# GpSimd issues the next expert's gather ahead of its wait for the last scatter; tokens loaded first and normalised by a diagonal product

## The reference, cut to what matters

```python
def _rmsnorm(x, gain):
    y = xf * lax.rsqrt(jnp.mean(xf * xf, axis=-1, keepdims=True) + EPS)
    return y * gain

def _layer(x, ...):
    xn = _rmsnorm(x, p['norm_mix'])
    z = xn @ p['w_in']                       # u | q | f | i | g
    y_s5 = ...                               # diagonal state space scan, GELU, GLU, RMSNorm
    y_hg = ...                               # 8 heads of 128x128 state, chunked
    x = x + concat([y_s5, y_hg]) @ p['w_out']
    return x + _hier_moe(_rmsnorm(x, p['norm_ffn']), ...)

def _hier_moe(x, w_coarse, b_coarse, w_fine, b_fine, w_gate, w_up, w_down):
    # top-1 group of 4, then top-2 of its 8 experts: gate (n, 32) has two entries per token
    hg = einsum('nd,edf->nef', xs, w_gate)   # 32 experts, 2048 -> 512
    hu = einsum('nd,edf->nef', xs, w_up)
    act = silu(hg) * hu * gate[:, :, None]
    return einsum('nef,efd->nd', act, w_down)
```

## Time and profile before

| | |
|---|---|
| median of 3 runs | 1835.31 us (1832.76 to 1837.85) |
| profiled execution, time | 1835.85 us |
| profiled execution, span | 1834.0 us, 19193 instructions |
| TensorE busy, weight load busy | 1483.5 us (81%), 908.7 us (50%) |
| VectorE, ScalarE, GpSimd busy | 599.6 us, 274.4 us, 308.3 us |
| moved by DMA | 505.26 MB, mean 275 GB/s |
| of it the expert weights | 192 loads of 2 MB |

### The profile page before, as it was taken

The page is one execution under the profiler, slowest core; times in us unless marked ns, Lnnn a source line. Parts: engine busy times, 40 slices in busy tenths (PEclk is TensorE's granted clock), DMA queues, the critical chain, the costliest instruction groups (busy, mean ns, idle before and its releaser), DMA issues.

```text
span 1834.0 us, 19193 instructions
## 1 busy us (share of the span) xinstructions
PE 1483.5 (81%) x7437; PEld 908.7 (50%) x7437; DVE 599.6 (33%) x1466; ACT 274.4 (15%) x501; POOL 308.3 (17%) x426
## 2 busy tenths in 40 slices
PE   6799988879988997778878788787887878878870
PEld 5676666567766875434434334333343334433330
DVE  2779999956654124101010010100101001010015
ACT  1100001143331001110111111111011111111111
POOL 0055555433310010000000000000000000000006
PEclk9999998999998998887978888788888888888885
DMA  9323322344514564699999999999999999999954
GB/s 281 121 93 99 129 89 81 109 138 131 165 38 112 183 230 165 248 410 384 403 390 386 385 397 395 388 388 393 386 382 403 382 394 400 395 391 394 389 222 151
DMA packets 130318, 505.26 MB, mean 275 GB/s; under 512 B 23716, under 2 KB 99700, under 8 KB 102780
## 3 DMA queue, kind: packets, MB, share of 16 engines
q1 hardware_dynamic: 112908, 493.74, 70.1%
q0 software_dynamic: 5200, 9.19, 1.5%
q10 hardware_dynamic: 12160, 1.67, 0.6%
HBM read 503.19 MB, written 26.28 MB: 289 GB/s over the span
## 4 chain that ended last, share of the span: by engine, by line
PE 31%; DMA 27%; issue 5%; ACT 3%; DVE 2%; POOL 1%; POOLq 0%; ACTq 0%; SPq 0%; DVEq 0%
PE bank L1288 16%; DMA arena<-x_rows,idx_tok 15%; DMA expert_rows<-arena,idx_dst 11%; PE bank L1197 6%; PE bank L1234 5%; ACT arena L726 3%; PE bank L1267 2%; PE bank L906 1%; DVE arena L1794 1%; DMA ring<-expert_rows 1%; PE bank L1164 0%; PE bank L1147 0%; POOL arena L868 0%; POOL arena L861 0%; PE bank L1175 0%
## 5 line engine op out<-in xcount | busy, mean ns | idle before, releaser
L1267 PE MATMUL bank<-ring,arena 128*64 128x512 f32 x2048 | 450.5, 595 | 0.0
L1267 PEld LDWEIGHTS bank<-ring,arena 128*64 128x64 f32 x2048 | 227.1, 137 | 195.2 <-issue 195.2
L1288 PE MATMUL bank<-ring,arena 128*64 128x512 f32 x1024 | 292.6, 736 | 19.0 <-DVE arena L1794 19.0
L1234 PE MATMUL bank<-ident,arena 64*128 64x64 f32 x721 | 96.9, 326 | 189.1 <-DMA arena<-x_rows,idx_tok 185.2
L936 PE MATMUL bank<-arena,ring 128*128 128x280 f32 x768 | 195.6, 416 | 4.5 <-ACT arena L576 3.1
L1789 DVE SCALAR_TENSOR_TENSOR arena<-arena,gcol 64x512 f32<-64x512 f32 x32 | 35.6, 1113 | 499.2 <-ACT arena L721 499.2
L1234 PEld LDWEIGHTS bank<-ident,arena 64*128 64x128 f32 x721 | 90.5, 242 | 217.5 <-DMA arena<-x_rows,idx_tok 212.5
L1288 PEld LDWEIGHTS bank<-ring,arena 128*64 128x64 f32 x1024 | 87.4, 171 | 201.9 <-issue 201.9
L936 PEld LDWEIGHTS bank<-arena,ring 128*128 128x128 f32 x768 | 150.4, 198 | 48.7 <-issue 8.7
L845 POOL DMA_INDIRECT expert_rows<-arena,idx_dst x32 | 29.5, 921 | 779.5 <-ACT arena L726 779.5
L726 ACT ACTIVATE arena<-bank 64x512 f32<-64x512 f32 x128 | 75.9, 593 | 527.2 <-PE bank L1288 526.1
(11 more groups left out here) (334 smaller groups left out, 1435.5 us busy)
## 6 DMA issues: line engine op xcount, KB each, us to landing
ring<-in_w_down_dram SPq DMA_DIRECT2D x64, 2048.0 KB, 9.0
ring<-in_w_gate_dram SPq DMA_DIRECT2D x64, 2048.0 KB, 9.5
ring<-in_w_up_dram SPq DMA_DIRECT2D x64, 2048.0 KB, 15.3
ring<-in_w_in_dram SPq DMA_DIRECT2D x20, 2048.0 KB, 8.7
ring<-in_w_out_dram SPq DMA_DIRECT2D x8, 2048.0 KB, 9.4
ring<-in_s_w_glu_dram SPq DMA_DIRECT2D x2, 2048.0 KB, 8.3
arena<-v_samples SPq DMA_DIRECT2D x8, 512.0 KB, 4.2
ring<-expert_rows SPq DMA_DIRECT2D x4, 1024.0 KB, 10.6
```

The source lines that it names most:

```text
L1234: return pe.matmul(out, rows, eye, start=True, stop=True) if waits else pe.transpose(out, rows, eye)
L1267: ins = pe.matmul(PB[b][at:at + CAP, :], xgT[b][:, kk, :], slot(s, KD // 2)[:, k, :], start=(kk == 0), stop=(kk == KD - 1))
L1288: ins = pe.matmul(PB[2 + cc // 2][at:at + CAP, :], hT[:, f, :], slot(4 + half, KF // 2)[:, k, cc * 512:(cc + 1) * 512], start=(f == 0), st ...
```

## The change

In the loop, GpSimd's wait for a scatter and the raise of `rows_free` move behind the next gather. For x: wait for `tr_done`, gather x+1, wait for scatter x-1, raise `rows_free`, wait for `rows_ready`, scatter x. The first pair is written out ahead of the loop, since it has no earlier scatter, and the last scatter is waited for behind the loop.

In the head, the tiles are taken in the order 0, 1, 2 and all loaded before the vectors. The sum of squares of a tile is made in two halves of 1024 columns, one by ScalarE, one by VectorE, and added by VectorE. The tile is no longer scaled: VectorE writes the reciprocals into a diagonal matrix `diag`, and TensorE multiplies by that in place of the transpose.

```diff
--- before.py
+++ after.py
@@ -194,6 +194,7 @@
         q_own = c(NH, NS, NS)
         assert c.at <= 2 * SLOT
         c = Carver(upair, 0)
+        diag = c(3, P)
         xsq = c(D)
         ang_r, ang_n, ang_cos, ang_sin = (c(NJ, 33) for _ in range(4))
         z_tmp = [c(NS, NJ), c(NS, NJ)]
@@ -245,6 +246,8 @@
         idx_tok = [sb(f"idx_tok{i}", [CAP, 1], U32) for i in range(2)]
         idx_dst = [sb(f"idx_dst{i}", [CAP, 1], U32) for i in range(2)]
         gcol = [sb(f"gcol{i}", [CAP, 1]) for i in range(2)]
+        half_sums = sb("half_sums", [P, 3, 2])
+        HALF_SQ = D // 2
         rcol = [sb(f"rcol{i}", [CAP, 1]) for i in range(2)]
         square_sums = sb("square_sums", [P, 3, D // CB])
 
@@ -264,7 +267,7 @@
         vec_loaded, s5_loaded, bc_loaded, wr_loaded = sems("vec_loaded s5_loaded bc_loaded wr_loaded")
         slot_loaded = [sem(f"slot_loaded{i}") for i in range(6)]
         pool_consts, dve_consts, act_step, dve_step, pool_step = sems("pool_consts dve_consts act_step dve_step pool_step")
-        x_rms, xn_made, xt_done, xt_copied, vec_t, vec_copied = sems("x_rms xn_made xt_done xt_copied vec_t vec_copied")
+        x_half, x_summed, x_rms, xn_made, xt_done, xt_copied, vec_t, vec_copied = sems("x_half x_summed x_rms xn_made xt_done xt_copied vec_t vec_copied")
         lb_in, lb_exp = sems("lb_in lb_exp")
         s5_exp_in, s5_exp, s5_sin_in, s5_sin, s5r_ready = sems("s5_exp_in s5_exp s5_sin_in s5_sin s5r_ready")
         par_t, par_copied, ang_ready, table_ready = sems("par_t par_copied ang_ready table_ready")
@@ -415,11 +418,10 @@
                     rows = t[name].rearrange("a (k p) -> (a k) p", p=P)
                     sp.dma_start(vrow[at:at + rows.shape[0], :], rows).then_inc(vec_loaded, 16)
 
-            for tile in TILE_ORDER:
+            for tile in range(3):
                 for at, rows in token_rows(tile):
                     sp.dma_start(xraw[at:at + rows.shape[0], tile, :], rows).then_inc(x_loaded[tile], 16)
-                if tile == TILE_ORDER[0]:
-                    load_vectors()
+            load_vectors()
             for n in range(NW + PRE_SLOTS):
                 pre_load(n)
 
@@ -536,19 +538,16 @@
                     act.dma_start(h0row[:, z, half, :], src[half].rearrange("b j n -> (b j) n")).then_inc(s5_loaded, 16)
             step = Chain(act, act_step)
 
-            def token_rms(src, scratch, tile, signal):
-
-                n = TT[tile]
-                s = token_stats[0:n, tile:tile + 1]
-                step.link(nc.scalar.activation(scratch[0:n, :], src[0:n, tile, :], ACT.Square, accum_out=s))
-                nc.scalar.activation(s, s, ACT.Sqrt, bias=eps_col[0:n, :], scale=1.0 / D).then_inc(signal, 1)
-
-
             act.wait_ge(dve_consts, 1)
             nc.scalar.activation(token_stats[:, 7:8], eps_col[:, :], ACT.Sqrt)
-            for tile in TILE_ORDER:
+            for tile in range(3):
+                n = TT[tile]
                 act.wait_ge(x_loaded[tile], 16 * len(token_rows(tile)))
-                token_rms(xraw, xsq, tile, x_rms)
+                nc.scalar.activation(xsq[0:n, 0:HALF_SQ], xraw[0:n, tile, 0:HALF_SQ], ACT.Square,
+                                     accum_out=half_sums[0:n, tile, 0:1]).then_inc(x_half, 1)
+                act.wait_ge(x_summed, tile + 1)
+                nc.scalar.activation(token_stats[0:n, tile:tile + 1], token_stats[0:n, tile:tile + 1], ACT.Sqrt,
+                                     bias=eps_col[0:n, :], scale=1.0 / D).then_inc(x_rms, 1)
             for z, (bn, cn) in enumerate((("s5_B_re", "s5_C_re"), ("s5_B_im", "s5_C_im"))):
                 act.dma_start(Braw[z], t[bn][0].rearrange("(j g) p c -> (g p) j c", g=2)).then_inc(bc_loaded, 16)
                 act.dma_start(Craw[z], t[cn][0].rearrange("(i g) c p -> (g c) i p", g=8)).then_inc(bc_loaded, 16)
@@ -829,24 +828,36 @@
                                         in_offset=bass.IndirectOffsetOnAxis(ap=idx_tok[p][:, 0:1], axis=0),
                                         bounds_check=last_token, oob_is_err=False).then_inc(gathered[p], 16)
 
+            def pair_of_rows(R, i, first):
+
+                for b in range(2):
+                    x = i * 2 + (R * NE + b)
+                    g = i * 2 + (R * (NE + 1) + b + 1)
+
+                    pool.wait_ge(tr_done, g)
+                    gather(g, 1 - b)
+
+                    if b == 1:
+                        pool.wait_ge(scattered[0], i * 16 + (R * (NE // 2) + 1) * 16)
+                        pool.sem_inc(rows_free, 1)
+                    elif not first:
+                        pool.wait_ge(scattered[1], i * 16 + R * (NE // 2) * 16)
+                        pool.sem_inc(rows_free, 1)
+                    pool.wait_ge(rows_ready, x + 2)
+                    pool.sem_inc(wait_carried, 1)
+                    pool.indirect_dma_start(out=y_dram, out_offset=bass.IndirectOffsetOnAxis(ap=idx_dst[b][:, 0:1], axis=0),
+                                            in_=yout[b][0:CAP, :], in_offset=None, bounds_check=last_row,
+                                            oob_is_err=False).then_inc(scattered[b], 16)
+
             def round_rows(R):
                 if not is_first(R):
                     pool.wait_ge(tr_done, R * (NE + 1) + 1)
                 gather(R * (NE + 1), 0)
-                with pool.Fori(0, NE // 2) as i:
-                    for b in range(2):
-                        x = i * 2 + (R * NE + b)
-                        g = i * 2 + (R * (NE + 1) + b + 1)
-
-                        pool.wait_ge(tr_done, g)
-                        gather(g, 1 - b)
-                        pool.wait_ge(rows_ready, x + 2)
-                        pool.sem_inc(wait_carried, 1)
-                        pool.indirect_dma_start(out=y_dram, out_offset=bass.IndirectOffsetOnAxis(ap=idx_dst[b][:, 0:1], axis=0),
-                                                in_=yout[b][0:CAP, :], in_offset=None, bounds_check=last_row,
-                                                oob_is_err=False).then_inc(scattered[b], 16)
-                        pool.wait_ge(scattered[b], i * 16 + (R * (NE // 2) + 1) * 16)
-                        pool.sem_inc(rows_free, 1)
+                pair_of_rows(R, 0, True)
+                with pool.Fori(1, NE // 2) as i:
+                    pair_of_rows(R, i, False)
+                pool.wait_ge(scattered[1], (R + 1) * (NE // 2) * 16)
+                pool.sem_inc(rows_free, 1)
 
             run_rounds(pool, round_rows)
             pool.engine_nop().then_inc(moe_done, 1)
@@ -886,7 +897,7 @@
             pe.transpose(PB[7][:, 0:80], vrow[0:80, :], ident[0:80, 0:80]).then_inc(vec_t, 1)
 
 
-            for i, tile in enumerate(TILE_ORDER):
+            for i, tile in enumerate(range(3)):
                 n = TT[tile]
                 pe.wait_ge(xn_made, i + 1)
                 for q in range(KD // 4):
@@ -895,7 +906,8 @@
                         pe.wait_ge(xt_copied, unit - 3)
                     for a in range(4):
                         k = 4 * q + a
-                        ins = pe.transpose(PB[unit % 4][:, a * P:a * P + n], xraw[0:n, tile, k * P:(k + 1) * P], ident[0:n, 0:n])
+                        ins = pe.matmul(PB[unit % 4][:, a * P:a * P + n], xraw[0:n, tile, k * P:(k + 1) * P], diag[0:n, tile, 0:n],
+                                        start=True, stop=True)
                     ins.then_inc(xt_done, 1)
 
             def last_tile(bank, lhs, w):
@@ -1303,17 +1315,36 @@
             nc.vector.memset(square_sums[:, :, :], 0.0)
             nc.vector.memset(eps_col[:, :], EPS).then_inc(dve_consts, 1)
 
-            for i, tile in enumerate(TILE_ORDER):
+            def sum_squares(tile):
+
                 n = TT[tile]
-                dve.wait_ge(x_rms, i + 1)
+                dve.wait_ge(x_loaded[tile], 16 * len(token_rows(tile)))
+                half = xraw[0:n, tile, HALF_SQ:D]
+                step.link(STT(xsq[0:n, HALF_SQ:D], half, 1.0, half, ALU.mult, ALU.mult, accum_out=half_sums[0:n, tile, 1:2]))
+                dve.wait_ge(x_half, tile + 1)
+                TTo(token_stats[0:n, tile:tile + 1], half_sums[0:n, tile, 0:1], half_sums[0:n, tile, 1:2], ALU.add) \
+                    .then_inc(x_summed, 1)
+
+            def make_diag(tile):
+
+                n = TT[tile]
+                dve.wait_ge(x_rms, tile + 1)
                 r = token_stats[0:n, 3 + tile:4 + tile]
                 step.link(nc.vector.reciprocal(r, token_stats[0:n, tile:tile + 1]))
-                TS(xraw[0:n, tile, :], xraw[0:n, tile, :], r, None, ALU.mult).then_inc(xn_made, 1)
+                TS(diag[0:n, tile, 0:n], ident[0:n, 0:n], r, None, ALU.mult).then_inc(xn_made, 1)
+
+            dve.wait_ge(pool_consts, 4)
+            sum_squares(0)
+            sum_squares(1)
+            make_diag(0)
+            sum_squares(2)
+            make_diag(1)
+            make_diag(2)
             dve.wait_ge(vec_t, 1)
```

(2 more changed lines are left out.)

## The result

The changed kernel takes 1804.71 us (median of 4 runs, 1800.81 to 1807.39) against 1836.58 us for the kernel before (4 runs, 1832.76 to 1840.75): a ratio of 0.9828, interval 0.9806 to 0.985. It is faster, by about half of what was forecast, and 1.7 us beyond the upper end of the range. The profiled execution has a span of 1805.5 us (its own time 1807.39), 28.5 less than the 1834.0 of before.

A forecast was written before the change was run, and what follows sets the result against it. TensorE's late gathered rows kept the weight queue from staying full. From a span of 1834.0 us, 49.2 (loop), 7.7 (loop's end) and 3.0 (head) were taken, giving 1774.1; with 1.3 added, 1775.4 us, range 1750 to 1803.

The forecast's parts named there:

- The mechanism and the order: Expert loop: gather issued while the scatter is in flight, so TensorE's row waits vanish and it waits for weights instead.
- The period: Expert loop: time per expert between last weight landings falls from 32.84 to 31.2 us, a gain of 49.2 us.
- The prediction's own sign of being wrong: Expert loop: landings staying 32 us and more per expert while TensorE waits for them would refute the forecast.
- the period is what the queue needs when it is full: Expert loop: the weight queue never runs low, so an expert takes 29.3 us plus the cost of the rows' traffic.
- what the rows' own traffic costs: Expert loop: gather and scatter traffic added to the loads' 29.3 us, bounded by totals of 30.25 and 32.0, taken as 31.2.
- the queue has less to give: Rival, expert loop: transfer starts, not TensorE's lateness, make the gaps; 31.8 to 32.4 us an expert, 1802 us; chance 0.19.
- The end of the loop: Loop's end: last scatter issued 10.9 us after the last weight landing instead of 18.65, gaining 7.7 us.
- w_down products at 7.1 us, at a clock near 1.0: Expert loop: expected sign in the profile after, TensorE's w_down products running at full clock in 7.1 us.
- The slow rival, the clock: Rival, expert loop: three new TensorE waits each drop the clock, costing 3 us each; 34 us an expert, 1870 us; chance 0.04.
- The rule that spoke against the change: Expert loop: HBM side binds at about 358 GB/s, six loads take an estimated 35 us, so the loop gains nothing.
- The head: Kernel's start: earlier token loads, split sum of squares and diagonal products gain 3.0 us, ends 0 and 4.5.
- first pause of the projections ending near 48 us: Head: expected sign, TensorE's first pause in the projections, waiting for ScalarE until 51.16 us before, ends near 48 us.

The follow-up runs named there:

- spread: Changed kernel with the first 16 rows of an expert's list laid at every second position, one to a DMA engine: 1785.92 us, ratio 0.9719.
- rotate: Changed kernel with rows at every second list position and every second expert's list starting eight DMA engines further on: 1776.71 us, ratio 0.9666.
- loop alone: The kernel before with only GpSimd's new order in the loop, old head: 1809.48 us, ratio 0.9861.
- without rows: Changed kernel with gather and scatter indices all out of bounds, transfers still issued but every row skipped: 1729.01 us.
- head alone: Changed kernel with GpSimd's old order in the loop, so only the new head remains: 1835.09 us, ratio 0.9992.
- the two kernels that fill rows ahead of the loop: Changed kernel with all gather and scatter rows skipped, 1729.01 us, and with only scatter rows skipped, 1792.13 us; result rows filled once beforehand.
- the last kernel: Changed kernel with TensorE's transpose of the vectors moved behind the first unit of diagonal products: 1810.83 us.
- packed: Changed kernel with list rows laid out so that four consecutive ranks share each DMA engine: 1849.39 us.
- the gather alone: Changed kernel with only the scatter's destinations out of bounds, result rows filled once before the loop: 1792.13 us.
- the scatter alone: Changed kernel with only the gather's row numbers out of bounds, so gathered rows are skipped: 1741.97 us.

## Why the prediction was right or wrong

**The mechanism and the order: right.** The gather's wait nearly gone (17.4 us of 168.0), waits for the up loads in its place, 1.23 us from scatter to gather issue (under 2 was forecast). The six loads at 29.46 us (29.3). The slices of the loop came out at 386 to 427 GB/s, not at 405 to 420 in every one.

**The period: the step that failed.** It is "I take 31.2: the third expert's 30.25, and 1 us for the gather that it did not have". It was 32.18, and 30 x 0.98 = 29.4 us of gain were missing. The prediction's own sign of being wrong is what came: landings 32 us and more apart while TensorE waits for them. "the period is what the queue needs when it is full" was nearly right; the term on top, "what the rows' own traffic costs", was put at 1.9 us and is 2.72. It was mis-sized in two ways. The base was one expert, and a light one: the gather beside its loads had 5 rows (packet records, 788 to 792 us), which say little of the mean of 17.5. And the trace of before held a tighter bound that was not read: in its loop the mean DMA engine was already at work for 94.8 + 2.7 = 97.5% of the time, and a full stretch of the same trace adds up to 101. All that a never-empty queue can give back is 3.5% of 32.84 us, 1.15 us, so, with the rows where they are, no period below 31.7 and a gain of at most 34 us over the loop. This takes the time on weights and rows as given; it fell by 0.13. The forecast took 49. It counted 1.64 of the 3.5 us above the floor as time in which the queue stood low (the 1.1 and a part of the 2.1), where it mostly worked: on rows, and on weights slowed by them. Only when rows and weights share it evenly does the idle part go (spread, rotate); in the changed kernel half of it stays, now as engines that wait for the most loaded one.

**The rival that came in** is "the queue has less to give", at 1802 us (1792 to 1812, chance 0.19), with its period of 31.8 to 32.4. Its reason was only half right: not the starts of transfers, but rows on uneven engines and slower packets.

**The end of the loop: the right chain, one term off.** Forecast 10.9 us from last landing to last scatter, measured 13.75 in this execution. The second up load landed 10.5 us ahead of the last w_down (10.3), then 7.09 (7.0), 3.9 (3.8), w_down's products 9.97 (7.1), 3.2 (3.3). The 2.9 us are the clock: the gate and up group behind the wait of 1.63 us still ran in 7.09 us, but then TensorE waited twice for VectorE, 1.31 and 0.59 us with five transposes between, and the granted clock in the products behind that was 0.70:

```profile
1747.00:1757.50 10.50, 9.97 (x32) 2.91 (x32) 1.56 (x3) 0.00 (x0) 0.00 (x0) 0.70 0.01 2
```

This is also where "w_down products at 7.1 us, at a clock near 1.0" was wrong: over the loop the mean is 8.67 us (277.4 / 32). It is not so at every loop's end: in the kernel with the loop alone the last w_down products took 7.09 us, and the last scatter stood 10.49 us behind the last landing, near the forecast's 10.9. Over the nine kernels with the new order this distance runs from 10.49 to 16.02 us, one execution each.

**The slow rival, the clock: its mechanism came, its price didn't.** There were up to three slow groups an expert. But in the expert shown each cost 1.6 to 1.8 us over 7.0, not 3: 25.0 + 3 x 1.8 = 30.4 us, under the loads' 32.18, so it decided nothing in the loop. In the mean of the loop gate and up take 2 x 7.59 us (486.0 / 64 a half) and w_down 8.67, 2.8 us over 13.93 and 7.09 together. The Trainium skill (TensorE: Matmul & The Clock Gate, HAM oscillation) describes a kernel that goes cold at every wait for a load. The trace agrees in part, with groups of 8.64 and 8.78 us behind waits of 2.40 and 3.75, but 7.09 behind the 1.63 us of the last expert.

**The rule that spoke against the change**, the Trainium skill's 358 GB/s (DMA: Bandwidth & Descriptors, Where 436 GB/s comes from), would have had the loads at an estimated 35 us an expert. The runs disagree: without rows the loads run at 427 GB/s over 800 us (341.86 MB), six in 29.46. Another page of the Trainium skill (Perfetto Trace Analysis, Roofline) gives some 435 GB/s as the bound that the DMA engines set for a lone active core. The 427 is consistent with that one. The upper limit of the loads was thus never in doubt, only what shares it.

**The head: 3.0 forecast, 3.05 seen, and not to be called right.** With the same head, the first scatter stands at 772.2, 773.9 (head alone), 773.1, 770.8, 769.5, 770.6 and 771.6 us (the two kernels that fill rows ahead of the loop left out); with the old one at 775.2 and 773.9 (loop alone). The means differ by 2.9 us, and runs of one head by up to 4.4. The time of the head alone, 0.9992 (0.9976 to 1.0008), gives -1.5 to 4.4 us. Of the steps, the B load goes out at 13.70 (11.1 to 13.5 forecast, 15.9 before), since the second full tile landed only at 10.5, and ScalarE comes to the banks at 48.91 (46.4 to 48.8). The products started at 14.08 and not at 11, behind the vectors' transpose, where the last kernel starts them at 12.26: that the vectors "are needed first when the banks are copied" missed that TensorE transposes them ahead of everything. The full ones took 0.31 us each (9.9 us for 32), near the dear end of 0.22 to 0.35, and the projections began at 29.28 (21.5 to 26). A part of that is the clock, which was 0.72 in 24 to 29 us: with the same head and the old loop all 48 products took 12.94 us instead of 14.76, at a clock of 1.00, and the projections began at 27.42. The "first pause of the projections ending near 48 us" did not come: TensorE was now the later one. What it lost there it got back near 80 us, where its wait for VectorE shrank from 6.12 to 1.78 us and the clock stayed up; with the head alone the same wait was 3.55 us.

**The sum.** Missing are 29.4 us in the loop and 2.8 at its end, less 0.6 behind it and nothing at the head: 31.6, against 59.9 - 28.5 = 31.4 us of span.

## What to carry to other kernels

Before a gain is claimed from a fuller queue, add up the shares of all queues in the DMA view of that stage and set the sum against a stretch in which the queue is full; only what lacks can be won by filling it, however large the gaps between landings look. Here a transfer of a short list of rows loaded some DMA engines and not others, and the large loads beside it landed later for it: spread the rows so that each engine gets one before any gets two, and start the next list elsewhere. To price such traffic, skip it in a kernel of its own and read the period; a light iteration of the loop is no base.

## What the runs showed of the hardware

- An indirect transfer of 8 KB rows starts about half of its rows at once (7 of 13), all when they stand at every second place of the list (13 of 13), a third when packed (4 of 13): neighbours in the list share a DMA engine. That the list always begins at the same engine is inferred from rotate. The same 560 rows each way took the loop's period from 31.13 us (spread and rotated) over 32.18 (as listed) to 33.61 (packed).
- Beside a full queue a gather of 17.5 rows costs 1.94 us and a scatter of as many 0.62 (one execution of each kernel). The gather slows the weights' packets: 98.0% of the engines' time for 322.55 MB with the gather alone, 99.2% for 336.73 MB with the scatter alone, that is 3.1% more per byte.
- A skipped row still costs a packet: with all rows skipped, 54 transfers had 4,320 packets, 80 each for 64 places of the list, of 4 bytes and 0.3% of the time.
- A float32 product with a 128-column diagonal took 0.31 us (9.9 us for 32; 0.29 in the kernel with the head alone), where a transpose of the same tile took 0.17 (5.58 us for 32).
